# An mLSTM layer's q/k preparation: two buffers, halves, and a place inside the previous head's pipeline

## The chip, the cores and the metric

The kernel runs on the 8 cores of one Trainium2 chip. Each core computes two of the sixteen sequences on its own; nothing is exchanged. The metric is device microseconds of the slowest core.

## The reference

One layer of a hybrid decoder and a last RMSNorm. For each sequence of 2048 rows, with 1024 features:

```
x = x + 1/2 * SwiGLU_1(RMSNorm(x))
h = RMSNorm(x)
p = h @ w_in               # q, k, v, o, gates of the mLSTM; q, k, v, gates of the sparse attention
y_mlstm                    # 4 heads of 128
y_nsa                      # 8 query heads of 64: compressed, selected and window branches
x = x + concat(y_mlstm, y_nsa) @ w_out
x = x + 1/2 * SwiGLU_2(RMSNorm(x))
out = RMSNorm(x)
```

What matters here is how q and k of an mLSTM head come about, and what they are used for:

```
qk = silu(causal_conv(concat([mq, mk]), conv_w))      # 4 taps along time, each channel on its own
s  = (q . k) / sqrt(128) * exp(decay), causal          # per head, 2048 x 2048, lower triangle
h  = (s @ v) / max(|sum of s|, exp(-m))                # then a norm per head, times sigmoid(mo)
```

## The kernel before

A small scheduler of the kernel's own (`Prog`) takes instructions with the buffers that they read and write (`Buf`: the last writer and the readers since), puts each at the end of its engine's list, and waits on semaphores where one engine needs another. The order in each engine's queue is thus the order of `emit` calls in the program, and nothing moves later.

A core goes through its two sequences one after the other. Each has a feed-forward part, the mixer and a second feed-forward part, with barriers between them. The mixer (L476) first projects gates, v (`Vp`) and o (`sigmo`), then runs the four mLSTM heads, then the sparse attention, then the output projection. The change touches the mLSTM heads (L577 to L726).

A head has two parts.

*Preparation* (L611 to L625), for q and then for k: `load_w` sends 128 columns of the weights through POOL's DMA queue into one of two `wb` buffers; `proj_fm` (L529) makes four groups of eight matmuls, one group for each 512 rows of time, each into a PSUM bank; ACT copies every bank to `qpre` (fp32, 2048 columns and 3 of padding). DVE computes the four convolution taps over all 2048 columns into `cacc` (L617 once, L621 three times). ACT applies SiLU and writes `qT` or `kT` (L624). There is one `qT`, one `kT`, one `qpre` and one `cacc`. All of it stands in the program ahead of the head's pipeline.

*Pipeline* (L626 to L726): time is cut into four blocks I of 512 query rows, and for block I there are 4I + 4 steps j, one for each 128 key rows: 4 + 8 + 12 + 16 = 40 steps. At a block's first step, PE broadcasts a row of the decay in fp32 (L635), ACT copies it to `nmb` (L639), and DVE clears two accumulator banks (L643). Each step (`ml_A`) is a score matmul (L649), an Exp on ACT into `wg` (L653, ring of 4), their product `pt` on DVE (L657), and for the four diagonal steps of a block a mask on POOL (L661). The value matmuls (`ml_C`, L673) of a step are emitted LOOK = 2 steps later. At a block's end DVE copies the accumulators out (L681), and four small stages follow: s1 on DVE, s2 four squares on ACT (L702), s3 Ln and Exp on ACT, s4 on DVE (L713, and L717 four times, into `mixcat`).

Those stages come through `defer(delay, fn)`: `run_pipeline` (L512) emits `ml_A` of step t, `ml_C` of step t - 2, and then calls `tick()`, which counts every deferred function down by one and emits those that reach zero, in the order in which they were deferred. There are 42 ticks for 40 steps; what is left is emitted at the end.

`nextbank` hands out the eight PSUM banks in turn and leaves out those that are held.

Of the kernel before, what the change touches and what calls it, by code (L numbers as in the profile page):

```python
# [6 lines left out]
F32 = mybir.dt.float32  # L7
# [8 lines left out]
T = 2048  # L16
# [220 lines left out]
def build_program(nseq, debug=(), do_mixer=True):  # L237
# [46 lines left out]
    with es:  # L284
# [186 lines left out]
        def dump(name, src_ap, reads):  # L471
            if name in dbg:
                P.final_ops.append(P.emit(POOL, lambda e: e.dma_start(out=dbg[name], in_=src_ap), reads=reads, dma=True))


        def mixer(s):  # L476
# [46 lines left out]
            def load_w(name, ncols, c0=0):  # L523
                t, b = wring.next()
                src = wd[name].rearrange("(k p) m -> p k m", p=128)[:, :, c0:c0 + ncols]
                pool_cast_load(t[:, :, 0:ncols], src, [b])
                return t, b

            def proj_fm(wt, wb, c0, M, evac):  # L529
                for tg in range(4):  # L530
                    bk, bb = nextbank()
                    for k in range(8):
                        P.emit(PE, lambda e, k=k, tg=tg, bk=bk: e.matmul(  # L533
                            bk[0:M, :], lhsT=wt[:, k, c0:c0 + M], rhs=hT[:, k, tg * 512:(tg + 1) * 512],
                            start=(k == 0), stop=(k == 7)), reads=[wb, B_hT[tg]], writes=[bb])
                    evac(tg, bk, bb)
# [55 lines left out]
            wt, wb = load_w("w_mo", 512)  # L592

            def ev_o(i, bk, bb):
                st, sb_ = sgring.next()
                P.emit(ACT, lambda e: e.activation(out=st[:], in_=bk[:, :], func=AF.Sigmoid), reads=[bb], writes=[sb_])
                P.emit(DVE, lambda e: e.tensor_tensor(out=sigmo[:, i, :], in0=st[:], in1=gnbc[:], op=ALU.mult),
                       reads=[sb_, B_const], writes=[B_sig[i]])
            proj_tm(wt, wb, 0, 512, ev_o)
            P.emit(ACT, lambda e: e.activation(out=rowA[:], in_=rowA[:], func=AF.Exp), reads=[B_rA], writes=[B_rA])  # L600
            for (row, B_row, tok, B_tok) in ((rowI, B_rI, ztok, B_zt), (rowA, B_rA, ecltok, B_et)):
# [5 lines left out]
                       reads=[bb], writes=[B_tok])  # L607


            for h in range(4):  # L610
                for (wname, dstT, B_dst, cbase) in (("w_mq", qT, B_qT, 0), ("w_mk", kT, B_kT, 4)):  # L611
                    wt, wb = load_w(wname, 128, c0=h * 128)
                    P.emit(DVE, lambda e: e.memset(qpre[:, 0:3], 0.0), writes=[B_qpre])
                    proj_fm(wt, wb, 0, 128, lambda tg, bk, bb: P.emit(ACT, lambda e: e.copy(
                        out=qpre[:, 3 + tg * 512:3 + (tg + 1) * 512], in_=bk[:, :]), reads=[bb], writes=[B_qpre]))
                    cw = convw[:, cbase + h, :]
                    P.emit(DVE, lambda e, cw=cw: e.tensor_scalar(out=cacc[:], in0=qpre[:, 3:3 + T], scalar1=cw[:, 3:4],  # L617
                                                                 scalar2=None, op0=ALU.mult),
                           reads=[B_qpre, B_const], writes=[B_cacc])
                    for j in (2, 1, 0):  # L620
                        P.emit(DVE, lambda e, cw=cw, j=j: e.scalar_tensor_tensor(  # L621
                            out=cacc[:], in0=qpre[:, j:j + T], scalar=cw[:, j:j + 1], in1=cacc[:],
                            op0=ALU.mult, op1=ALU.add), reads=[B_qpre, B_cacc, B_const], writes=[B_cacc])
                    P.emit(ACT, lambda e, dstT=dstT: e.activation(out=dstT[:], in_=cacc[:], func=AF.Silu),  # L624
                           reads=[B_cacc], writes=[B_dst])  # L625
                steps = []  # L626
                for I in range(4):
                    st_I = {}
# [3 lines left out]
                def ml_A(I, j, st, h=h):  # L632
                    if j == 0:
# [8 lines left out]
                        for ab_, abb_ in accb:  # L642
# [6 lines left out]
                    P.emit(PE, lambda e, bs=bs: e.matmul(bs[:, c0:512], lhsT=kT[:, j * 128:(j + 1) * 128],  # L649
                                                         rhs=qT[:, I * 512 + c0:(I + 1) * 512], start=True, stop=True),  # L650
                           reads=[B_kT, B_qT], writes=[bbs])
# [77 lines left out]
            dump("d_qT", qT[:], [B_qT])  # L729
            dump("d_kT", kT[:], [B_kT])  # L730
            dump("d_nm", rowL[:], [B_rL])
            P.barrier()
            ar.reset(m_ar1)
# [453 lines left out]
```

How the kernel before makes its waits and increments, by code:

```python
    def replay(self, engname, eng):  # L127
        sems = self.sem_handles
        cur_wait = {}
        def wait(d):
            if cur_wait.get(d.sem, 0) >= d.val:
                return
            cur_wait[d.sem] = d.val
            eng.wait_ge(sems[d.sem], d.val)
        for op in self.ops[engname]:
            if op.is_dma and op.dma_prev is not None:
                wait(op.dma_prev)
            for d in op.deps.values():
                wait(d)
            if op.fn is None:
                continue
            ins = op.fn(eng)
            if op.is_dma:
                ins.then_inc(sems[op.sem], 16)
            elif op.waited:
                ins.then_inc(sems[op.sem], 1)
        if engname == SP:
            for o in self.final_ops:
                wait(o)
```

## Time and profile before

| | us |
|---|---|
| median of 3 runs | 5117.03 (5116.47 to 5202.21) |
| the profiled execution | 5112.91 |
| its span on the slowest core (core 7) | 5111.3 |
| spans of all cores | 5098.6 to 5111.3 |
| PE busy in the span | 3625.7 (71%) |
| DVE busy | 2238.9 (44%) |
| ACT busy | 1556.2 (30%) |
| POOL busy | 200.6 (4%) |

Times in the rows are microseconds from the first instruction of the span, on core 7. A busy time of an engine counts the time in which it executes; the end of a matmul is modelled, and matmuls overlap, so a busy PE is not a full PE. A row of a timeline merges neighbouring instructions of one form; in brackets stands how long the engine had been idle, and whose semaphore ended that. PEclk is the TensorE clock that was granted, as a share of 2.4 GHz.

### The profile page before, as it was taken

The numbers are of one execution on the slowest core, as the hardware profiler recorded it, in microseconds if no ns is written. First come the engines' busy times: TensorE is split into PE (matmuls) and PEld (weight loads), VectorE is DVE, ScalarE is ACT, GpSimd is POOL, SyncE is SP. The second block draws the span as 40 slices with busy tenths as digits, with TensorE's granted clock in tenths as the row PEclk, the third lists the DMA queues.
The fourth block names the chain that finished last, engine by engine and source line by source line (L and its number), as shares of the span: only waits on it lengthen the run. The fifth ranks groups of instructions, "written<-read, shape, count | busy, mean of one in ns | idle before, by whom it ended". The sixth has DMA issues, their size and how long they took to land.

```text
span 5111.3 us, 64455 instructions; the slowest of 8 cores (5098.6 to 5111.3 us)
## 1 busy us (share of the span) xinstructions
PE 3625.7 (71%) x19360; PEld 1709.4 (33%) x19360; DVE 2238.9 (44%) x5530; ACT 1556.2 (30%) x3053; POOL 200.6 (4%) x294
## 2 busy tenths in 40 slices
PE   3999474558575745999549993755595757459995
PEld 2444132224232323444224441322252323234442
DVE  2434335550575733343524343355506757333434
ACT  3110234441363633101130102344413636331011
POOL 0000000010000000000000000000100000000000
PEclk9999685666656558999869996856675565679997
DMA  5321110002000033130422201100110000331301
GB/s 120 42 34 25 70 21 5 5 5 31 9 2 5 1 83 58 26 50 13 97 89 42 33 13 70 21 5 5 14 23 8 1 5 1 83 58 25 50 13 66
DMA packets 147758, 169.65 MB, mean 33 GB/s; under 512 B 48828, under 2 KB 118460, under 8 KB 147424
## 3 DMA queue, kind: packets, MB, share of 16 engines
q0 software_dynamic: 124224, 101.78, 13.6%
q1 hardware_dynamic: 23200, 63.74, 3.6%
q8 instruction: 170, 2.79, 0.2%
q14 instruction: 164, 1.34, 0.1%
HBM read 225.33 MB, written 33.55 MB: 51 GB/s over the span
## 4 chain that ended last, share of the span: by engine, by line
PE 58%; DVE 16%; ACT 9%; issue 8%; DMA 7%; DVEq 1%; POOL 0%; ACTq 0%; SPq 0%; POOLq 0%
PE bank L444 12%; PE bank L448 12%; PE bank L462 11%; PE bank L533 5%; PE bank L542 3%; PE bank L978 3%; PE bank L1057 2%; PE bank L805 2%; DVE cacc L621 2%; PE bank L1011 2%; DVE hnacc L853 2%; ACT pt L986 2%; DMA xstash<-xs 2%; ACT nj L384 2%; ACT wg L653 1%
## 5 line engine op out<-in xcount | busy, mean ns | idle before, releaser
L452 ACT ACTIVATE sil<-bank 128x512 f32<-128x512 f32 x352 | 210.1, 597 | 1541.9 <-PE bank L444 1541.9
L454 DVE TENSOR_TENSOR aT<-sil,bank 128x512 bf16<-128x512 f32 x352 | 242.0, 687 | 984.8 <-PE bank L448 959.8
L444 PE MATMUL bank<-hT,w1g 128*128 128x512 bf16 x2816 | 669.9, 381 | 0.0
L448 PE MATMUL bank<-hT,w3g 128*128 128x512 bf16 x2816 | 665.3, 379 | 0.0
L462 PE MATMUL bank<-w2g,aT 128*128 128x512 bf16 x2816 | 622.6, 379 | 6.9 <-DVE xs L465 6.5
L465 DVE SCALAR_TENSOR_TENSOR xs<-bank,xs 128x512 f32<-128x512 f32 x768 | 524.1, 691 | 119.4 <-PE bank L462 82.5
L986 ACT ACTIVATE pt<-bank 128x512 bf16<-128x512 f32 (+3 forms) x1088 | 465.5, 504 | 283.3 <-PE bank L978 194.2
L396 PE MATMUL bank<-ident_b,nh 128*128 128x128 bf16 x768 | 97.1, 306 | 445.2 <-DVE nh L390 444.9
L462 PEld LDWEIGHTS bank<-w2g,aT 128*128 128x128 bf16 x2816 | 271.0, 98 | 354.6 <-issue 38.4
L444 PEld LDWEIGHTS bank<-hT,w1g 128*128 128x128 bf16 x2816 | 276.7, 98 | 334.4 <-issue 5.4
L448 PEld LDWEIGHTS bank<-hT,w3g 128*128 128x128 bf16 x2816 | 275.6, 98 | 332.6 <-issue 0.6
L533 PE MATMUL bank<-hT,wb 128*128 128x512 bf16 (+2 forms) x1408 | 337.4, 405 | 49.6 <-DMA wb<-w_mq 26.9
L649 PE MATMUL bank<-qT,kT 128*128 128x512 bf16 (+1 forms) x320 | 167.3, 539 | 171.6 <-ACT kT L624 146.3
L1011 PE MATMUL bank<-VV,pt 128*128 128x65 bf16 x3296 | 274.4, 234 | 8.6 <-DVE pt L989 3.6
L673 PE MATMUL bank<-Vp,pt 128*128 128x129 bf16 x1088 | 165.3, 294 | 156.8 <-DVE pt L657 126.2
L657 DVE SCALAR_TENSOR_TENSOR pt<-bank,wg 128x512 bf16<-128x512 f32 (+1 forms) x320 | 185.8, 608 | 184.2 <-ACT wg L653 114.8
L1011 PEld LDWEIGHTS bank<-VV,pt 128*128 128x128 bf16 x3296 | 185.7, 120 | 180.9 <-issue 166.5
L396 PEld LDWEIGHTS bank<-ident_b,nh 128*128 128x128 bf16 x768 | 74.3, 138 | 468.8 <-issue 468.8
L978 PE MATMUL bank<-nqT,ksdT 64*128 64x512 bf16 (+3 forms) x640 | 181.9, 497 | 63.2 <-DVE sm L842 35.0
L533 PEld LDWEIGHTS bank<-hT,wb 128*128 128x128 bf16 (+2 forms) x1408 | 145.2, 104 | 236.5 <-issue 93.5
L1057 PE MATMUL bank<-wout,mcT 128*128 128x512 bf16 x512 | 119.5, 388 | 128.1 <-DMA wout<-w_out 86.1
L653 ACT ACTIVATE wg<-nmb,ztok 128x512 bf16<-128x512 f32 (+1 forms) x320 | 190.3, 647 | 17.9 <-DVE pt L657 12.6
(164 smaller groups left out, 3420.8 us busy)
## 6 DMA issues: line engine op xcount, KB each, us to landing
w1g<-ffn_w POOLq DMA_DIRECT2D x20, 1024.0 KB, 10.8
w3g<-ffn_w POOLq DMA_DIRECT2D x20, 1024.0 KB, 14.9
w2g<-ffn_w POOLq DMA_DIRECT2D x20, 1024.0 KB, 8.8
xs<-x SPq DMA_DIRECT2D x32, 512.0 KB, 13.7
xstash<-xs SPq DMA_DIRECT2D x32, 512.0 KB, 2.7
out<-fo SPq DMA_DIRECT2D x32, 512.0 KB, 2.7
xs<-xstash SPq DMA_DIRECT2D x16, 512.0 KB, 14.6
xs<-xstash POOLq DMA_DIRECT2D x16, 512.0 KB, 18.1
```

Source lines behind the costliest of these rows:

```text
L444: P.emit(PE, lambda e, k=k, fc=fc, tg=tg, bu=bu, t1=t1: e.matmul(bu[:, :], lhsT=t1[:, k, fc * 128:(fc + 1) * 128], rhs=hT[:, k, tg * 512:( ...
L448: P.emit(PE, lambda e, k=k, fc=fc, tg=tg, bv=bv, t3=t3: e.matmul(bv[:, :], lhsT=t3[:, k, fc * 128:(fc + 1) * 128], rhs=hT[:, k, tg * 512:( ...
L452: P.emit(ACT, lambda e, bu=bu, st=st: e.activation(out=st[:], in_=bu[:, :], func=AF.Silu), reads=[bbu], writes=[sbf])
L454: P.emit(DVE, lambda e, fc=fc, tg=tg, st=st, bv=bv: e.tensor_tensor(out=aT[:, fc, tg * 512:(tg + 1) * 512], in0=st[:], in1=bv[:, :], op=AL ...
L462: P.emit(PE, lambda e, fc=fc, i=i, half=half, by=by, t2=t2, nfc=nfc: e.matmul(by[:, :], lhsT=aT[:, fc, i * 128:(i + 1) * 128], rhs=t2[:, f ...
L465: P.emit(DVE, lambda e, i=i, half=half, by=by: e.scalar_tensor_tensor(out=xs[:, i, half * 512:(half + 1) * 512], in0=by[:, :], scalar=0.5, ...
L533: P.emit(PE, lambda e, k=k, tg=tg, bk=bk: e.matmul(bk[0:M, :], lhsT=wt[:, k, c0:c0 + M], rhs=hT[:, k, tg * 512:(tg + 1) * 512], start=(k = ...
L653: P.emit(ACT, lambda e, wg=wg, nmb=nmb: e.activation(out=wg[:, c0:512], in_=nmb[:, c0:512], func=AF.Exp, bias=ztok[:, j, h:h + 1], scale=1.0),
L978: P.emit(PE, lambda e, bs=bs, r0=r0: e.matmul(bs[:, c0:c1], lhsT=kTt[r0:r0 + 64, j * 128:(j + 1) * 128], rhs=nqT[r0:r0 + 64, p, I * 512 + ...
L986: P.emit(ACT, lambda e, pt=pt, bs=bs: e.activation(out=pt[:, c0:c1], in_=bs[:, c0:c1], func=AF.Exp, scale=SC_N), reads=[bbs], writes=[pb])
L1011: P.emit(PE, lambda e, ab=ab, q=q, pt=pt, i=i: e.matmul(ab[:, q * 65:(q + 1) * 65], lhsT=pt[:, q * 128:(q + 1) * 128], rhs=VV[:, j, vidx, ...
L1057: P.emit(PE, lambda e, k=k, half=half, by=by, mc=mc: e.matmul(by[:, :], lhsT=mc[:, k, :], rhs=wout[:, k, half * 512:(half + 1) * 512], sta ...
```

## The change

The two parts of a head are taken apart. `prep_sched(h)` makes a list of small functions, each with an offset, that together are the preparation of head h. For head 0 they are all emitted ahead of the loop. For heads 1 to 3 they are deferred, by their offset plus 2 ticks, when the pipeline of head h - 1 begins, so that they are emitted between its steps.

- `qT` and `kT` have two buffers each; head h uses number h % 2.
- `cacc` has 1024 columns in place of 2048. Each convolution and each SiLU is done in two halves, one after the other, in the one `cacc`.
- The banks of the projection are held from the matmuls to their copy, one tick later.
- `wg` has 3 buffers in place of 4, and `sg` is gone: the sigmoid of o goes through the first 512 columns of `cacc`.

```diff
             qpre = arx.alloc("qpre", [128, T + 3], F32)
-            cacc = arx.alloc("cacc", [128, T], F32)
-            qT = arx.alloc("qT", [128, T], BF16)
-            kT = arx.alloc("kT", [128, T], BF16)
-            B_qpre, B_cacc, B_qT, B_kT = Buf(), Buf(), Buf(), Buf()
-            wgring = Ring(arx, "wg", [128, 512], BF16, 4)
-            sgring = Ring(arx, "sg", [128, 512], F32, 1)
+            cacc = arx.alloc("cacc", [128, T // 2], F32)
+            qTb = [arx.alloc(f"qT{i}", [128, T], BF16) for i in range(2)]
+            kTb = [arx.alloc(f"kT{i}", [128, T], BF16) for i in range(2)]
+            B_qTb = [Buf(), Buf()]
+            B_kTb = [Buf(), Buf()]
+            B_qpre, B_cacc = Buf(), Buf()
+            wgring = Ring(arx, "wg", [128, 512], BF16, 3)
...
+            def prep_sched(h):
+                par = h % 2
+                sched = []
+                base = 0
+                for (wname, dstT, B_dst, cbase) in (("w_mq", qTb[par], B_qTb[par], 0), ("w_mk", kTb[par], B_kTb[par], 4)):
+                    hold = {}
+                    cw = convw[:, cbase + h, :]
...
+                        hold["w"] = load_w(wname, 128, c0=h * 128)
+                        P.emit(DVE, lambda e: e.memset(qpre[:, 0:3], 0.0), writes=[B_qpre])
+                    sched.append((base, p_load))
+                    for tg in range(4):
...
+                        sched.append((base + 1 + tg, p_mm))
+                        sched.append((base + 2 + tg, p_ev))
+                    for hf in range(2):
+                        o = hf * (T // 2)
+                        s0 = base + (6 if hf == 0 else 11)
...
+                        sched.append((s0, p_c0))
+                        for n_, j in enumerate((2, 1, 0)):
...
+                            sched.append((s0 + 1 + n_, p_cj))
...
+                        sched.append((s0 + 4, p_silu))
+                    base += 17
+                return sched
+
+            for _, fn in sorted(prep_sched(0), key=lambda t: t[0]):
+                fn()
             for h in range(4):
...
+                if h + 1 < 4:
+                    for off, fn in prep_sched(h + 1):
+                        defer(off + 2, fn)
```

`p_mm` is the eight matmuls of one 512-row group, `p_ev` ACT's copy to `qpre`, `p_c0` the first tap (a tensor_scalar over 1024 columns), `p_cj` one of the three others, `p_silu` the SiLU of 1024 columns. The score matmul reads `kTb[h % 2]` and `qTb[h % 2]`.

## Rows read from the trace of the kernel before

**Rows 1.** the page's slices: granted TensorE clock in tenths, 127.8 us each

```profile
PEclk9999685666656558999869996856675565679997
```

**Rows 2.** wait list, 747 to 1141 us: waiter, releaser, us, times, longest us

```profile
PE bank L649 <- ACT kT L624: 73.2, 4, 18.6
...
DVE pt L657 <- ACT wg L653: 58.1, 38, 3.6
```

**Rows 3.** windows: us, busy PE, PEld, DVE, ACT, POOL; clock, DMA

```profile
747.06:781.79 34.73, 16.52 (x67) 6.89 (x67) 17.95 (x13) 9.81 (x12) 0.00 (x0) 0.75 0.00 0
781.79:841.18 59.39, 37.08 (x181) 18.67 (x181) 34.26 (x83) 33.71 (x75) 6.23 (x16) 0.55 0.00 1
846.50:852.50 6.00, 5.91 (x14) 2.11 (x15) 1.31 (x6) 0.74 (x2) 0.00 (x0) 0.50 0.24 24
852.50:857.00 4.50, 4.50 (x22) 2.06 (x21) 0.00 (x0) 1.46 (x3) 0.00 (x0) 1.00 0.01 4
```

**Rows 4.** timeline of ACT: start us, us, engine, line, operation [idle before, releaser]

```profile
779.74 1.91 ACT L624 ACTIVATE kT<-cacc 128x2048 bf16<-128x2048 f32 x1 [8.85 <-DVE cacc L621]
781.55 0.57 ACT L639 COPY nmb<-bank 128x512 f32<-128x512 f32 x1
782.20 1.28 ACT L653 ACT_TABLE_LOAD   x1
...
829.22 0.71 ACT L653 ACTIVATE wg<-nmb,ztok 128x512 bf16<-128x512 f32 x1
...
1079.28 1.91 ACT L624 ACTIVATE kT<-cacc 128x2048 bf16<-128x2048 f32 x1 [8.86 <-DVE cacc L621]
```

**Rows 5.** groups of instructions: busy us, mean ns, idle before

```profile
L452 ACT ACTIVATE sil<-bank 128x512 f32<-128x512 f32 x352 | 210.1, 597 | 1541.9 <-PE bank L444 1541.9
...
L390 DVE SCALAR_TENSOR_TENSOR nh<-xs,rstd,gbc 128x1024 bf16<-128x1024 f32 x96 | 119.3, 1282 | 140.7 <-DMA gbc<-mix_norm 80.9 <-DMA gbc<-ffn_norm 53.0 <-DVE rstd L376 3.5
...
L621 DVE SCALAR_TENSOR_TENSOR cacc<-qpre,convw,cacc 128x2048 f32<-128x2048 f32 x48 | 112.9, 2352 | 5.4 <-DVE cacc L617 0.5
...
L617 DVE TENSOR_SCALAR cacc<-qpre,convw 128x2048 f32<-128x2048 f32 x16 | 20.6, 1287 | 115.5 <-ACT qpre L614 115.5
```

**Rows 6.** timeline of DVE in head 0, columns as in rows 4

```profile
784.32 1.49 DVE L657 SCALAR_TENSOR_TENSOR pt<-bank,wg 128x512 bf16<-128x512 f32 x3 [3.55 <-ACT wg L653]
...
797.05 0.69 DVE L657 SCALAR_TENSOR_TENSOR pt<-bank,wg 128x512 bf16<-128x512 f32 x1 [2.37 <-ACT wg L653]
...
801.38 1.03 DVE L643 MEMSET bank<- 128x512 f32 x2
...
805.72 1.30 DVE L657 SCALAR_TENSOR_TENSOR pt<-bank,wg 128x512 bf16<-128x512 f32 x2 [3.31 <-PE bank L649]
...
823.68 1.30 DVE L657 SCALAR_TENSOR_TENSOR pt<-bank,wg 128x512 bf16<-128x512 f32 x2 [2.43 <-ACT wg L653]
...
830.09 0.69 DVE L657 SCALAR_TENSOR_TENSOR pt<-bank,wg 128x512 bf16<-128x512 f32 x1 [2.37 <-ACT wg L653]
...
833.05 2.72 DVE L657 SCALAR_TENSOR_TENSOR pt<-bank,wg 128x512 bf16<-128x512 f32 x4
...
836.87 0.69 DVE L657 SCALAR_TENSOR_TENSOR pt<-bank,wg 128x512 bf16<-128x512 f32 x1 [0.17 <-DVE pt L657]
...
840.68 0.29 DVE L657 SCALAR_TENSOR_TENSOR pt<-bank,wg 128x128 bf16<-128x128 f32 x1 [0.51 <-PE bank L649]
...
847.11 1.14 DVE L717 SCALAR_TENSOR_TENSOR mixcat<-accs,sm,sigmo 128x128 bf16<-128x128 f32 x4
```

**Rows 7.** timeline of POOL: first masks of head 0, load for head 1

```profile
785.16 1.26 POOL L661 TENSOR_TENSOR pt<-pt,trile 128x128 bf16<-128x128 bf16 x3 [42.04 <-DVE pt L657]
...
841.67 0.94 POOL L341 DMA_DIRECT2D wb<-w_mq  x1
```

**Rows 8.** timeline of PE: a row broadcast and the projections of head 1

```profile
819.83 2.07 PE L635 MATMUL bank<-rowL,sel 4*128 4x512 f32 x2
...
846.59 11.70 PE L533 MATMUL bank<-hT,wb 128*128 128x512 bf16 x40 [4.68 <-DMA wb<-w_mq]
```

More of the change, by code:

```diff
@@ L594, in ev_o @@
             def ev_o(i, bk, bb):
[L595 to L598, printed above, removed]
+                P.emit(ACT, lambda e: e.activation(out=cacc[:, 0:512], in_=bk[:, :], func=AF.Sigmoid), reads=[bb], writes=[B_cacc])
+                P.emit(DVE, lambda e: e.tensor_tensor(out=sigmo[:, i, :], in0=cacc[:, 0:512], in1=gnbc[:], op=ALU.mult),
+                       reads=[B_cacc, B_const], writes=[B_sig[i]])
             proj_tm(wt, wb, 0, 512, ev_o)
@@ L607, in mixer @@
                        reads=[bb], writes=[B_tok])
-            for h in range(4):
[L611 to L625, printed above, removed]
@@ new lines, in prep_sched, with p_load, p_mm, p_ev @@
+            def prep_sched(h):
[5 more added lines that the diff above has]
+                    cw = convw[:, cbase + h, :]
+                    def p_load(wname=wname, hold=hold):
+                        hold["w"] = load_w(wname, 128, c0=h * 128)
+                        P.emit(DVE, lambda e: e.memset(qpre[:, 0:3], 0.0), writes=[B_qpre])
+                    sched.append((base, p_load))
+                    for tg in range(4):
+                        def p_mm(tg=tg, hold=hold):
+                            wt, wb = hold["w"]
+                            bk, bb = nextbank(hold=True)
+                            for k in range(8):
+                                P.emit(PE, lambda e, k=k: e.matmul(
+                                    bk[:, :], lhsT=wt[:, k, 0:128], rhs=hT[:, k, tg * 512:(tg + 1) * 512],
+                                    start=(k == 0), stop=(k == 7)), reads=[wb, B_hT[tg]], writes=[bb])
+                            hold[("bk", tg)] = (bk, bb)
+                        def p_ev(tg=tg, hold=hold):
+                            bk, bb = hold[("bk", tg)]
+                            P.emit(ACT, lambda e: e.copy(out=qpre[:, 3 + tg * 512:3 + (tg + 1) * 512], in_=bk[:, :]),
+                                   reads=[bb], writes=[B_qpre])
+                            release(bb)
+                        sched.append((base + 1 + tg, p_mm))
[3 more added lines that the diff above has]
+                        s0 = base + (6 if hf == 0 else 11)
+                        def p_c0(o=o, cw=cw):
+                            P.emit(DVE, lambda e: e.tensor_scalar(out=cacc[:], in0=qpre[:, o + 3:o + 3 + T // 2], scalar1=cw[:, 3:4],
+                                                                  scalar2=None, op0=ALU.mult),
+                                   reads=[B_qpre, B_const], writes=[B_cacc])
+                        sched.append((s0, p_c0))
+                        for n_, j in enumerate((2, 1, 0)):
+                            def p_cj(o=o, cw=cw, j=j):
+                                P.emit(DVE, lambda e: e.scalar_tensor_tensor(
+                                    out=cacc[:], in0=qpre[:, o + j:o + j + T // 2], scalar=cw[:, j:j + 1], in1=cacc[:],
+                                    op0=ALU.mult, op1=ALU.add), reads=[B_qpre, B_cacc, B_const], writes=[B_cacc])
+                            sched.append((s0 + 1 + n_, p_cj))
+                        def p_silu(o=o, dstT=dstT, B_dst=B_dst):
+                            P.emit(ACT, lambda e: e.activation(out=dstT[:, o:o + T // 2], in_=cacc[:], func=AF.Silu),
+                                   reads=[B_cacc], writes=[B_dst])
+                        sched.append((s0 + 4, p_silu))
+                    base += 17
+                return sched
@@ L648, in ml_A @@
                     bs, bbs = nextbank()
-                    P.emit(PE, lambda e, bs=bs: e.matmul(bs[:, c0:512], lhsT=kT[:, j * 128:(j + 1) * 128],
-                                                         rhs=qT[:, I * 512 + c0:(I + 1) * 512], start=True, stop=True),
-                           reads=[B_kT, B_qT], writes=[bbs])
+                    P.emit(PE, lambda e, bs=bs: e.matmul(bs[:, c0:512], lhsT=kTb[h % 2][:, j * 128:(j + 1) * 128],
+                                                         rhs=qTb[h % 2][:, I * 512 + c0:(I + 1) * 512], start=True, stop=True),
+                           reads=[B_kTb[h % 2], B_qTb[h % 2]], writes=[bbs])
                     wg, wgb = wgring.next()
```

4 lines of the change are left out of this document (2 added, 2 removed).

## The prediction

> **What bounds the kernel now.** The page's clock row comes first [rows 1]: the change touches slices 6 to 9 and 26 to 29, where TensorE's granted clock is 5 or 6 tenths. Those are the mLSTM heads of the two sequences (four heads each, eight in all). The wait list over one sequence's heads comes next [rows 2]. The longest wait of PE with useful work behind it is for kT, the last piece of a head's preparation (73.2 us over four heads, 18 us each). Then the windows [rows 3]: the preparation of head 0 takes 34.7 us, its pipeline of 40 score steps 59.4 us. In the pipeline DVE is busy 34.3, ACT 33.7 and PE 37.1 us, and the clock is 0.55. So nobody is full, and DVE's idle 25 us look like room for the next head's preparation. The first kT and the last kT of the sequence start at 779.74 and 1079.28 [rows 4]: a head's period is 299.5/3 = 99.85 us. Of it, DVE's first to last score product (pt, 784.32 to 840.97) is 56.65 us [rows 6]; the other 43.2 us are handover, load, projection, convolution and SiLU.
>
> The timelines tell what sort of idle time it is. All five queues run in program order, and the program goes in lockstep: score matmul, wg on ACT, pt on DVE, then the value matmul two steps later. In the dense end of a head a step takes 0.86 us (0.69 of pt and 0.17 of wait at 836.87 [rows 6]), at the half clock nearly what PE needs for it. DVE's idle lies in lumps: about 3.3 us at the start of each 512-row block, and 2.37 us for wg behind four squares [rows 6].
>
> **The change, part by part.** I number the steps of a head 0 to 41. Blocks start at 0, 4, 12 and 24. The offsets plus 2 put the work here: q load after step 1; q matmuls after 2 to 5; q convolution, half by half, after 7 to 10 and 12 to 15; its SiLUs after 11 and 16; k load after 18; k matmuls after 19 to 22; k convolution after 24 to 27 and 29 to 32; SiLUs after 28 and 33. It applies to 3 heads of 4, so to 6 of 8. I follow the engine that releases pt, on the times of head 0.
>
> Removed: the 43.2 us between the last pt and the next first pt, in six places.
>
> Handover. What is left is the tail: accs, squares, Ln, Exp, four mixcat products end at 848.25, 7.3 us after the last pt; then two memsets of the next block's banks, queued behind them on DVE, 1.03 us [rows 6]. The new first pt comes 8.4 us after the last one.
>
> q load and projection. POOL works in order, and the load is queued behind the masks of steps 0 and 1. They start at 785.16, 0.84 after the first pt, and end at 786.0, 1.7 after it. From such a load's start to PE's first matmul on it is 846.59 - 841.67 = 4.9 us [rows 7, 8]; PE is in order too, so score matmul 3 waits behind the first projection matmul, and DVE runs dry. The burst now: 14 matmuls in 5.91 us at clock 0.50 (the 1.2 GHz level), the 26 after them in the rest of 11.70 us, 0.22 us each [rows 3, 8]. So 32 matmuls, the fp32 row broadcast of 2.07 us [rows 8] and some 1.7 us of score and value matmuls (diagonal ones, under two dense steps) are 13.5 + 2.1 + 1.7 = 17.3 us at half clock; 5.9 us pass at it and the rest goes twice as fast: 11.6 us. Then the last copy to qpre (0.6), the squares (2.4) and wg (0.9) come before pt 7: 3.9. Sum 1.7 + 4.9 + 11.6 + 3.9 = 22.1 from first pt to pt 7, against 797.05 - 784.32 = 12.7 now: +9.4. Block 1's own broadcast, copy and wg, which fill that stretch now, run under the burst.
>
> Costs of the halves. No row has 1024 fp32 columns of this operation from SBUF but the norm's, 1.28 us; half of the 2048-column one is 1.18 [rows 5]. I take 1.26 from start to start. The first tap is 0.64 (half of 1.287) to 1.29; I take 0.73, plus 0.1 between instructions. SiLU of 1024 columns: between 0.60 for 512 and 1.91 for 2048 [rows 4, 5], 1.03 by the line through them.
>
> First half of q (steps 7 to 11). DVE gets 0.5 more at step 7 (0.34 idle takes some) and 1.26 after each of the steps 8 to 10. The last tap ends about 805.6, with pt 11 still to come. ACT then needs table load 1.28, SiLU 1.03, nmb 0.58, the load back to Exp 1.28 [rows 4], and 0.87 from wg's start to pt's (829.22 to 830.09 [rows 4, 6]), with small gaps: pt 12 starts at 810.7, not 805.72. +5.0, nearly all of it the taps, since the boundary's idle covers the first load.
>
> Second half of q and first half of k (steps 12 to 16, 24 to 28: the same pattern). From 823.68: the first tap delays by 0.8, the second, ahead of the squares, by 1.3; the third hides in the 2.37 us wait; the fourth ends 2.1 after pt 27 starts, at 834.1. SiLU waits for it, then 1.28 + 1.03 + 1.28 + 0.87 and gaps give pt 29 at 838.7, against 833.05 [rows 6]: +5.7, twice. Behind the waiting SiLU on ACT stand wg 29 and after, and DVE waits for them; its only cover is pt 28 and the mixcat products.
>
> k load and projection (18 to 22). POOL has no mask from 12 to 19, so this load hides wholly (if not, 4.9 more). 32 matmuls and four dense steps are 13.5 + 3.4 = 16.9 to 17.1 at half clock, by the same burst 11.5 in fact, against 3.4 now: +8.1. Less 1.0, since the next broadcast runs at the higher clock: +7.1.
>
> Second half of k (29 to 33). There is no idle time here: +0.8 and three times 1.3, then DVE waits for the whole SiLU group but for one pt. From pt 29 to pt 34: 11.9 against 836.87 - 833.05 = 3.8: +8.1.
>
> Sum: 56.65 + 8.4 + 9.4 + 5.0 + 5.7 + 7.1 + 5.7 + 8.1 = 106.05 us, 6.2 above 99.85; six times, +37. The first head's preparation, now in halves over a single cacc, gains nothing and waits for SiLU at each half: +1.4, twice. Ring wg from 4 to 3: nothing, since wg is late for order and not for room [rows 2]; cacc in place of sg: nothing, one buffer each. So +40 us on the profiled 5112.9 (its span 5111.3 and 1.6 around it) is 5153; the median of the runs is 4 above that execution: 5157, and I say 5155. The work is interleaved, but each piece goes to a step where its engine is, or becomes, the last one.
>
> The Trainium skill ("ScalarE: Activation LUTs", section "What ACT_TABLE_LOAD costs") says that a switch of sets drains for 1.38 us on top of the load. This change makes 52 switches of 16; by that page the sum would be some 50 us higher, 5205. The row speaks against it: nmb ends at 782.12, the load starts at 782.20 and takes 1.28 [rows 4]. Its rule to batch calls by set is what the interleaving gives up; the load alone is in my terms.
>
> **The rivals.**
> Hidden after all (faster). The added 41 us per head fall into DVE's 25 us of idle time. For it: no engine is over 63% busy in the pipeline, and DVE waits 58 us for wg over four heads [rows 2, 3]. Against it: order within queues, above. If half of the 41 us vanish, the period is 85.5 and the time 5155 - 123 = 5032; with 30 hidden 76, and 4975. It decides from 23 us hidden per head (5155 to 5015 is 140 us, 23 a head). Below 5015: 0.10; between 5015 and 5080: 0.07.
> The clock stays down (slower). Both bursts start after starved stretches, and the pipeline's clock is 0.55 [rows 3]. If neither is raised, 17.2 in place of 11.6, twice a head: +11.2, +67 us, 5222. Against it: the burst of now rose after 14 matmuls [rows 3]. It decides where both bursts of all six heads stay low. 0.09. The other way, both at full clock from the start, is 3 us less per burst, 5119, inside the likeliest case.
> A switch of tables amid a full queue costs twice its row: 36 more at 1.28, +46, 5201. 0.04. This is the mechanism of the page named above.
> Likeliest: interleaved and not hidden, 5080 to 5215 with the last rival in it: 0.74; the middle of it, 5120 to 5190, 0.5.
>
> **How the numbers follow.** 5155 is the likeliest case. Range 5080 to 5215 leaves 0.17 below and 0.09 above; I take the low end down to 5060 for a few us per head of cover that I missed. Faster by over 2% is below 5015, slower above 5219; 2% is about what a measurement tells from no change. 0.11 faster, 0.79 within, 0.10 slower.
>
> **What would show it.** First pt to first pt about 106 us in three of four heads. Right if: DVE waits about 8 us for score matmul 3 behind a PE wait on w_mq after step 1; ACT shows 52 table loads and four DVE waits of 2 to 4 us per head behind them; the w_mk wait is gone; a DVE busier than 50 us per head. Wrong if the period is under 95: then taps or bursts were covered; over 112: then the bursts show clock 0.5 throughout, or a tap takes over 1.3 us.

## The result, and the profile after

| | before | after |
|---|---|---|
| profiled execution, us | 5112.91 | 5140.29 |
| its span on the slowest core | 5111.3 | 5138.7 |
| ratio, 95% interval | | 1.0051 (1.0037 to 1.0065) |

The change costs half a per cent, some 26 us. Executions in which the cores of a die ran slower at a lower clock are left out of every ratio and interval here; the others lie at 5114 to 5118 us before and at 5140 to 5145 after.

The page of the changed kernel, its span and its clock slices, against [rows 1]:

```profile
span 5138.7 us, 64577 instructions; the slowest of 8 cores (5123.8 to 5138.7 us)
...
PEclk9999685656656558999869996866566565579997
```

The clock pattern is that of before to a tenth or two: the change lives in slices 6 to 9 and 26 to 29 only. The wait list of core 3, the slowest, over the four heads of one sequence, 747 to 1170 us, against [rows 2] (waiter, releaser, us, times, longest):

```profile
DVE pt L699 <- ACT wg L695: 82.1, 40, 4.0
...
PE bank L691 <- ACT kT L656: 22.1, 1, 22.1
...
PE bank L627 <- DMA wb<-w_mq: 13.2, 3, 4.4
```

What the change says it does, it does: PE waits for kT once and not four times (22.1 us, before 73.2). But DVE's wait for wg has gone up from 58.1 to 82.1 us, and the wait for w_mq, 4.4 us a head, is still there. The windows of the first two overlapped periods, first pt to first pt (us, then busy PE, PEld, DVE, ACT, POOL; clock, DMA), against [rows 3]:

```profile
788.62:890.86 102.24, 52.53 (x248) 23.38 (x248) 54.47 (x114) 54.63 (x106) 11.35 (x18) 0.62 0.06 6
890.86:993.11 102.25, 52.67 (x248) 23.43 (x248) 54.44 (x115) 53.73 (x104) 11.40 (x18) 0.62 0.06 6
```

No engine is over 54% busy, and the period is 102.2 us where it was 99.3 to 101.0 in the three overlapped heads of that sequence. The work of two stretches is in one, and it takes as long as the two did. The same marks in DVE's timeline as in [rows 6]: first pt, pt 7, 12, 17, 24, 29, 34, the last one, and the next head's first:

```profile
788.62 1.50 DVE L699 SCALAR_TENSOR_TENSOR pt<-bank,wg 128x512 bf16<-128x512 f32 x3 [2.75 <-ACT wg L695]
...
811.10 0.69 DVE L699 SCALAR_TENSOR_TENSOR pt<-bank,wg 128x512 bf16<-128x512 f32 x1 [2.51 <-ACT wg L695]
...
824.16 0.69 DVE L699 SCALAR_TENSOR_TENSOR pt<-bank,wg 128x512 bf16<-128x512 f32 x1 [3.84 <-ACT wg L695]
...
839.05 1.91 DVE L699 SCALAR_TENSOR_TENSOR pt<-bank,wg 128x512 bf16<-128x512 f32 x3 [2.65 <-ACT wg L695]
...
852.75 0.69 DVE L699 SCALAR_TENSOR_TENSOR pt<-bank,wg 128x512 bf16<-128x512 f32 x1 [1.33 <-ACT wg L695]
...
867.27 0.69 DVE L699 SCALAR_TENSOR_TENSOR pt<-bank,wg 128x512 bf16<-128x512 f32 x1 [2.65 <-ACT wg L695]
...
878.56 1.99 DVE L699 SCALAR_TENSOR_TENSOR pt<-bank,wg 128x512 bf16<-128x512 f32 x3 [3.96 <-ACT wg L695]
...
882.20 0.29 DVE L699 SCALAR_TENSOR_TENSOR pt<-bank,wg 128x128 bf16<-128x128 f32 x1 [0.41 <-PE bank L691]
...
890.86 1.48 DVE L699 SCALAR_TENSOR_TENSOR pt<-bank,wg 128x512 bf16<-128x512 f32 x3
```

From these marks, [rows 6] and one more line of DVE's timeline before, that of pt 17:

```profile
815.10 1.88 DVE L657 SCALAR_TENSOR_TENSOR pt<-bank,wg 128x512 bf16<-128x512 f32 x3
```

All in us. The last column has the same marks over all six overlapped heads, after less before, on average:

| stretch | before | after | difference | forecast | mean of six heads |
|---|---|---|---|---|---|
| pt 0 to 7: q load and matmuls | 12.7 | 22.5 | +9.8 | +9.4 | +10.0 |
| 7 to 12: first half of q | 8.7 | 13.1 | +4.4 | +5.0 | +4.3 |
| 12 to 17: second half of q | 9.4 | 14.9 | +5.5 | +5.7 | +5.2 |
| 17 to 24: k matmuls | 8.6 | 13.7 | +5.1 | +7.1 | +6.2 |
| 24 to 29: first half of k | 9.4 | 14.5 | +5.2 | +5.7 | +5.2 |
| 29 to 34: second half of k | 3.8 | 11.3 | +7.5 | +8.1 | +7.5 |
| 34 to the end of the last pt | 4.1 | 3.9 | -0.2 | 0 | -0.1 |
| from there to the next head's first pt | 43.2 on average | 8.4 | -34.8 | -34.8 | -35.4 |

Head 0 is not typical in one row: its stretch 17 to 24 took 8.6 us before, and that of the five other heads 7.3 to 8.4; the mean of all six is 7.7. Over the six overlapped heads the sum is +18 us (mean period 99.7 before, 102.6 after); the two first heads' preparation adds 7 and all the rest 2: 27, the difference of the two spans.

### The profile page after: what moved, and what is told of

It reads as the page before. It is cut to its first block, busy times and chain, and to the rows that moved or that the text cites. A ratio compares the mean times of both kernels' runs of the same rounds, so it can differ in the third digit from the quotient of the medians.

```text
span 5138.7 us, 64577 instructions; the slowest of 8 cores (5123.8 to 5138.7 us)
## 1 busy us (share of the span) xinstructions
PE 3624.2 (71%) x19360; PEld 1699.0 (33%) x19360; DVE 2242.4 (44%) x5594; ACT 1604.3 (31%) x3105; POOL 218.3 (4%) x294
## 4 chain that ended last, share of the span: by engine, by line
PE 58%; DVE 15%; ACT 10%; issue 8%; DMA 7%; DVEq 1%; POOL 0%; ACTq 0%; SPq 0%; POOLq 0%
PE bank L444 12%; PE bank L448 12%; PE bank L462 11%; PE bank L533 4%; PE bank L542 3%; PE bank L1020 3%; PE bank L1099 2%; PE bank L847 2%; PE bank L1053 2%; PE bank L627 2%; DVE hnacc L895 2%; DVE cacc L650 2%; ACT pt L1028 2%; DMA xstash<-xs 2%; ACT nj L384 2%
## 5 line engine op out<-in xcount | busy, mean ns | idle before, releaser
L715 PEld LDWEIGHTS bank<-Vp,pt 128*128 128x128 bf16 x1088 | 99.3, 122 | 402.8 <-issue 392.0
L1020 PE MATMUL bank<-nqT,ksdT 64*128 64x512 bf16 (+3 forms) x640 | 181.3, 498 | 61.8 <-DVE sm L884 35.4
L533 PE MATMUL bank<-hT,wb 128*128 128x512 bf16 (+2 forms) x896 | 206.8, 395 | 22.7 <-DMA wb<-w_nq 11.8
L691 PE MATMUL bank<-qT,kT 128*128 128x512 bf16 (+1 forms) x320 | 157.1, 507 | 55.4 <-ACT kT L656 43.8
## 6 DMA issues: line engine op xcount, KB each, us to landing
w1g<-ffn_w POOLq DMA_DIRECT2D x20, 1024.0 KB, 11.5
```

The lines of the kernel that those rows point to most:

```text
L533: P.emit(PE, lambda e, k=k, tg=tg, bk=bk: e.matmul(bk[0:M, :], lhsT=wt[:, k, c0:c0 + M], rhs=hT[:, k, tg * 512:(tg + 1) * 512], start=(k = ...
L715: P.emit(PE, lambda e, ab=ab, o0=o0, pt=pt, q=q: e.matmul(ab[:, o0:o0 + 129], lhsT=pt[:, q * 128:(q + 1) * 128], rhs=Vp[:, j, h, 0:129], s ...
L1020: P.emit(PE, lambda e, bs=bs, r0=r0: e.matmul(bs[:, c0:c1], lhsT=kTt[r0:r0 + 64, j * 128:(j + 1) * 128], rhs=nqT[r0:r0 + 64, p, I * 512 + ...
```

## The experiments

Two views stand against each other. The order theory says that each piece costs by its place in an in-order queue: what it delays is read from the next pt. The rivals say that one thing eats the gain (table switches, the low clock, contention between engines), or that the pieces lie in idle time and the loss comes from elsewhere. The period of a run is the mean of first pt to first pt over its six overlapped heads.

### The halves alone

```diff
-            for _, fn in sorted(prep_sched(0), key=lambda t: t[0]):
-                fn()
             for h in range(4):
-                if h + 1 < 4:
-                    for off, fn in prep_sched(h + 1):
-                        defer(off + 2, fn)
+                for _, fn in sorted(prep_sched(h), key=lambda t: t[0]):
+                    fn()
```

> The halves alone, in the old order: every head's preparation stands ahead of its own pipeline again, but with cacc of 1024 columns, a convolution and a SiLU for each half, and wg with 3 buffers. The order theory (each piece of the new kernel costs by the place in its queue, and the halves have a price of their own) expects the price seen in the first head of the changed kernel, +3.8 us from ecltok to the first pt, at all 8 heads: +31 us, ratio 1.006 to before. The rival, that halves are as cheap as the whole and the slowdown comes from the interleaving alone, expects under +5 us, ratio 1.001.

Measured: ratio 1.0059 (1.0036 to 1.0082). A window over its first head's period:

```profile
787.26:889.95 102.69, 53.08 (x248) 25.05 (x248) 56.24 (x115) 46.77 (x99) 8.45 (x18) 0.63 0.06 6
```

102.7 us, and 103.1 on average: within half a us the period of the changed kernel. So what the change loses against before is what its halves cost, 3.4 us a head where they stand in the open, and the overlap as such is worth nothing: it takes 35 us off the gap and puts 37 into the pipeline. This run also has the three wg buffers. They are not what costs: from first pt to the end of the last a head takes 55.9 us on average here as before, and all the difference is between pipelines, 47.1 us against 43.8.

### The load of q ahead of the pipeline

```diff
-                        hold["w"] = load_w(wname, 128, c0=h * 128)
+                        hold["w"] = early.pop(h) if wname == "w_mq" and h in early else load_w(wname, 128, c0=h * 128)
...
                 if h + 1 < 4:
+                    early[h + 1] = load_w("w_mq", 128, c0=(h + 1) * 128)
                     for off, fn in prep_sched(h + 1):
```

> The changed kernel with one load moved: the next head's q weights are asked for ahead of the pipeline and not behind POOL's masks of steps 0 and 1. The order theory expects the 4.4 us for which PE waits for w_mq in every overlapped head to vanish whole, since DVE runs dry behind it: -4.4 x 6 = -26 us, about the time of before, ratio 1.000 (0.998 to 1.002). The rival, that this wait is covered by POOL, ACT and the drain of block 0, expects the time of the changed kernel, ratio 1.005.

Measured: ratio 1.0007 (0.9982 to 1.0031), period 98.9. PE's timeline in head 0 shows the first value matmuls and the q burst right behind them:

```profile
788.58 0.59 PE L718 MATMUL bank<-Vp,pt 128*128 128x129 bf16 x4 [2.94 <-DVE pt L702]
788.97 3.62 PE L629 MATMUL bank<-hT,wb 128*128 128x512 bf16 x8
```

The wait is gone, and 3.7 us a head with it, of the 4.4 expected.

### No table switch

```diff
-                            P.emit(ACT, lambda e: e.activation(out=dstT[:, o:o + T // 2], in_=cacc[:], func=AF.Silu),
+                            P.emit(ACT, lambda e: e.activation(out=dstT[:, o:o + T // 2], in_=cacc[:], func=AF.Silu if h == 0 else AF.Identity),
```

> The changed kernel with Identity in place of SiLU in the overlapped heads, so that no activation table is switched there (this leaves the SiLU of six heads out of the computation); all places and sizes stay. The order theory expects per head three groups shorter by the two table loads, 2.57 us, and the one at the block boundary by 2.1: -9.8 us a head, -59 us, 5084, ratio 0.994. The rival that the table switches are what eats the gain expects the overlap to pay once they are gone: over 17 us a head, below 5040, ratio 0.985 or less. The rival that they lie in ACT's idle time expects under 10 us in all.

Measured: ratio 0.9939 (0.9915 to 0.9963), period 92.8: -9.8 us a head, as worked out from the places. The switches are a quarter of what the pipeline got longer by (37 us, the table's rows but the last), not the whole of it.

### One tap of four

```diff
-                        for n_, j in enumerate((2, 1, 0)):
+                        for n_, j in enumerate((2, 1, 0) if h == 0 else ()):
```

> The changed kernel with only the first of the four taps in the overlapped heads (three quarters of their convolution are left out): 12 DVE instructions of 1.27 us less per head, 15.3 us of DVE time. The order theory expects most of it to be on the path, with the SiLUs no longer waiting for the last tap as well: -4.4, -3.3, -3.3 and -5 us in the four halves, -16 us a head, -96 us, 5047, ratio 0.986. The rival that the taps lie mostly in DVE's idle time, as its 44 per cent of busy time suggests, expects under -6 us a head, over 5105, ratio above 0.998.

Measured: 5080 us in a single execution (no interval), period 92.9, so -9.7 us a head and not -16, between my figure and the rival's. 15.3 us of DVE work came off; over a third of it did not shorten the period. The first fence is DVE's timeline at pt 17, the second ACT's there:

```profile
835.44 1.91 DVE L699 SCALAR_TENSOR_TENSOR pt<-bank,wg 128x512 bf16<-128x512 f32 x3 [2.40 <-ACT wg L695]
```

```profile
830.94 1.28 ACT L656 ACT_TABLE_LOAD   x1
832.24 1.06 ACT L656 ACTIVATE qT<-cacc 128x1024 bf16<-128x1024 f32 x1
833.31 1.28 ACT L695 ACT_TABLE_LOAD   x1
834.61 2.56 ACT L695 ACTIVATE wg<-nmb,ztok 128x512 bf16<-128x512 f32 x4
```

SiLU waits for no tap now, and starts as soon as wg 16 is done. Still it stands ahead of wg 17, and DVE waits 2.40 us for that, against 2.65 with the taps. The taps and the SiLU group are two chains of nearly one length; with one gone, the other sets pt 17. My expectation let both go at once.

### One matmul of eight

```diff
-                            for k in range(8):
+                            nk = 8 if h == 0 else 1
+                            for k in range(nk):
...
-                                    start=(k == 0), stop=(k == 7)), reads=[wb, B_hT[tg]], writes=[bb])
+                                    start=(k == 0), stop=(k == nk - 1)), reads=[wb, B_hT[tg]], writes=[bb])
```

> The changed kernel with one matmul of eight in each projection group of the overlapped heads (seven eighths of their projection are left out), 56 matmuls less per head. The order theory expects about 5 us less in the q burst and 5 in the k burst, the lengthening that the changed kernel's trace shows against before, less what the load's wait already covers: -10 us a head, -60 us, 5083, ratio 0.993. The rival that the bursts are hidden under ACT and DVE expects under 2 us a head, ratio above 1.002. The rival that the lower clock makes them dear expects more than 17 us a head.

Measured: ratio 0.9933 (0.9910 to 0.9957), period 93.0: -9.6 us a head. The wait for the weights stays, 4.85 us in PE's timeline:

```profile
793.98 0.59 PE L628 MATMUL bank<-hT,wb 128*128 128x512 bf16 x1 [4.85 <-DMA wb<-w_mq]
```

With seven eighths of the overlapped projection gone, all but 10 us of a 103 us period is still there. The projection is not the bound, and the low clock under it is not what eats the gain. The score and value matmuls still ran at the low clock; what a higher one would give them, no run shows.

### One SiLU group

```diff
-                            def p_cj(o=o, cw=cw, j=j):
+                            def p_cj(o=o, cw=cw, j=j, dstT=dstT, B_dst=B_dst):
+                                dst = cacc[:] if j else dstT[:, o:o + T // 2]
                                 P.emit(DVE, lambda e: e.scalar_tensor_tensor(
-                                    out=cacc[:], in0=qpre[:, o + j:o + j + T // 2], scalar=cw[:, j:j + 1], in1=cacc[:],
...
+                                    out=dst, in0=qpre[:, o + j:o + j + T // 2], scalar=cw[:, j:j + 1], in1=cacc[:],
...
-                            P.emit(ACT, lambda e: e.activation(out=dstT[:, o:o + T // 2], in_=cacc[:], func=AF.Silu),
-                                   reads=[B_cacc], writes=[B_dst])
-                        sched.append((s0 + 4, p_silu))
...
+                        P.emit(ACT, lambda e: e.activation(out=dstT[:], in_=dstT[:], func=AF.Silu),
+                               reads=[B_dst], writes=[B_dst])
+                    sched.append((32, p_silu))
```

> The full computation: the last tap writes q or k in bf16, and SiLU is applied in place, q and k together after step 33, so 2 table loads per overlapped head in place of 8. The order theory expects -3.2 us at step 11, -2.65 at steps 16 and 28 each, +2.8 after step 33 where the one group is 6.5 us long, in sum -5.7 us a head, -34 us, and -3 for the first heads, whose convolution waits for no SiLU now: 5106, ratio 0.998. The rival that the number of switches is what costs expects -6 x 1.28 us a head and more, -46 us or more beside the first heads: below 5095.

Measured: ratio 0.9964 (0.9946 to 0.9982), 5094 to 5095 us, period 95.7: -6.9 a head, and the first head's preparation is 3.5 to 4 us shorter. The time is the rival's figure (below 5095) as much as mine plus a miss of 12; this run alone does not tell the number of switches from their places, and it also lets a half's taps start without waiting for the SiLU of the half before. The run without switches prices the loads: 8 of them, all gone, gave 9.8.

### Load and tail

Against the run before:

```diff
-                    sched.append((32, p_silu))
+                    sched.append((38, p_silu))
...
+                    early[h + 1] = load_w("w_mq", 128, c0=(h + 1) * 128)
```

> The full computation: the early q load and the in-place SiLUs of the two runs before, with the SiLU group emitted after step 39 and not 33, where ACT has been seen idle for 4.8 us between the last wg and the squares. The order theory expects -26 (load), -37 (one group), and about -5 us a head for the place, -30: 5050, ratio 0.987. The rival that only the amount of work on an engine counts and not its place expects the last step to bring nothing: 5080, ratio 0.993.

Measured: ratio 0.9881 (0.9861 to 0.9900), period 89.0. That is 6.7 below 95.7: by the marks, the stretch with the q load is 5.0 shorter and pt 29 to 34, which held the SiLU group, 3.6, and the handover is 2.0 longer. If the load is worth its 3.7 here too, the place of the SiLU group is worth 3.0 and not the 5 expected. ACT's timeline at a head's end:

```profile
862.02 1.28 ACT L659 ACT_TABLE_LOAD   x1
863.32 1.91 ACT L659 ACTIVATE qT<-qT 128x2048 bf16<-128x2048 bf16 x1
865.13 1.89 ACT L659 ACTIVATE kT<-kT 128x2048 bf16<-128x2048 bf16 x1
866.93 0.39 ACT L748 ACTIVATE mjunk<-accs,sm 128x128 f32<-128x128 f32 x1
...
869.25 1.28 ACT L753 ACT_TABLE_LOAD   x1
```

The group begins when the last wg is done. The squares' input is ready at 866.15 and they start at 866.93: the group holds them up by 0.7 us or so. With the load back, 1.28 us and now ahead of Ln, that makes the handover 10.3 us and not 8.4.

### Slots for everything

The same pieces as in the run before, each after a step behind which the traces show its engine idle. The k load goes ahead of the pipeline too, qpre is tracked by quarters, so that a tap waits for the copies it reads and no others, and its first three columns are cleared once a sequence and not once a projection:

```diff
-                        sched.append((base + 1 + tg, p_mm))
-                        sched.append((base + 2 + tg, p_ev))
+            MM = {"w_mq": [0, 1, 4, 6], "w_mk": [12, 14, 16, 18]}
+            TAPS = [3, 3, 3, 6, 11, 11, 11, 14, 23, 23, 23, 26, 26, 28, 30, 32]
+            SILU = 39
...
+                        sched.append((s, p_mm))
+                        sched.append((s + 1, p_ev))
```

> The full computation, with every piece put where the trace shows its engine idle: both loads ahead of the pipeline; q matmuls after steps 0, 1, 4 and 6, k matmuls after 12, 14, 16 and 18; taps in threes after steps 3, 11 and 23 (block boundaries, DVE idle for 3.3 us) and single ones after 6, 14 and 26 (behind them the wait for the squares), the last three after 28, 30 and 32; q and k SiLU in place after step 39; qpre tracked by its four column groups. The order theory expects a head's period of pipeline 56.7, handover 8.4, exposed SiLU 1.6, exposed taps 5, half of the k burst 3.5 and some 3 of rest: 78 us against 99.85, -22 x 6 = -131 us: 4985, ratio 0.974 (0.968 to 0.982). The rival that overlap on this chip is lost to contention between engines whatever the place expects 5050 or more, as in the run before.

Measured: ratio 0.9688 (0.9669 to 0.9707), 4952 to 4954 us, period 75.2. Not all of it comes from places: in the first heads, where nothing overlaps, the finer tracking and the early k load take 6 us off the preparation against the run before. A window over one period:

```profile
854.08:927.92 73.84, 49.32 (x248) 22.36 (x247) 54.82 (x114) 45.25 (x97) 10.76 (x18) 0.73 0.08 8
```

DVE is at 74% and does as much as in the changed kernel (54.8 us against 54.5). Its timeline at the boundary to block 2 shows three taps and two memsets where there was a wait, and pt 12 right behind them:

```profile
872.09 0.74 DVE L651 TENSOR_SCALAR cacc<-qpre,convw 128x1024 f32<-128x1024 f32 x1
872.94 2.69 DVE L658 SCALAR_TENSOR_TENSOR cacc<-qpre,convw,cacc 128x1024 f32<-128x1024 f32 x2
875.73 1.02 DVE L697 MEMSET bank<- 128x512 f32 x2
876.66 0.67 DVE L711 SCALAR_TENSOR_TENSOR pt<-bank,wg 128x512 bf16<-128x512 f32 x1
```

### The old order with early loads

```diff
-                    wt, wb = load_w(wname, 128, c0=h * 128)
+                    wt, wb = early.pop(wname) if wname in early else load_w(wname, 128, c0=h * 128)
...
+                if h + 1 < 4:
+                    for wname in ("w_mq", "w_mk"):
+                        early[wname] = load_w(wname, 128, c0=(h + 1) * 128)
```

> The kernel of before with one thing moved: the next head's two weight loads are asked for ahead of the pipeline, the preparation stays where it was. The order theory expects PE's wait of 4.7 us for w_mq to vanish in the six later heads, since nothing else lies behind it there: -28 us, ratio 0.9945. So a part of what the slots kernel gains needs no overlap at all. The rival, that the tail of the head before (squares, Ln, Exp, mixcat) sets the start of the preparation anyway, expects under 2 us a head, ratio 0.998 or more.

Measured: ratio 0.9950 (0.9930 to 0.9969), period 95.1. PE's timeline between two heads, 64 projection matmuls right behind the last value matmul:

```profile
842.57 15.66 PE L533 MATMUL bank<-hT,wb 128*128 128x512 bf16 x64
```

Against [rows 8], where PE idled for 4.68 us before them. Two loads moved in the kernel of before do better than the whole change (0.9950 against 1.0051).

### Matmuls in slots, taps in rows

Against the slots kernel. One group of k's matmuls stands a step later, too:

```diff
-            MM = {"w_mq": [0, 1, 4, 6], "w_mk": [12, 14, 16, 18]}
+            MM = {"w_mq": [0, 1, 4, 6], "w_mk": [12, 15, 16, 18]}
-            TAPS = [3, 3, 3, 6, 11, 11, 11, 14, 23, 23, 23, 26, 26, 28, 30, 32]
+            TAPS = [7, 8, 9, 10, 12, 13, 14, 15, 24, 25, 26, 27, 29, 30, 31, 32]
```

> The slots kernel with its taps back at one per step (after steps 7 to 10, 12 to 15, 24 to 27, 29 to 32, as in the changed kernel), its matmuls still after 0, 1, 4, 6 and 12, 15, 16, 18, early loads and the SiLU group after step 39. It splits the 13.7 us a head between the run with early load and tail SiLU (period 88.9) and the slots kernel (75.2). The order theory expects the taps' places to be worth about 3.3 us idle at each of three block boundaries less what is lost in the memsets behind, 7 to 8 us, and the matmuls' places the rest, 6: period 83, about 5015, ratio 0.980. The rival that only the matmuls' places count, since PE with its low clock is the one that starves the others, expects the slots kernel's time, ratio 0.969.

Measured: ratio 0.9736 (0.9717 to 0.9756), 4976 to 4978 us, period 78.5. A window over one period:

```profile
858.38:936.20 77.82, 49.99 (x247) 23.26 (x251) 54.29 (x114) 46.59 (x98) 11.30 (x18) 0.70 0.07 8
```

So of the 13.8 us between 89.0 and 75.2 the matmuls' places (with the early k load and the finer tracking of qpre) are worth 10.5 and the taps' 3.3 (with that one group a step apart). I had given the taps 7 to 8; the rival gave all to the matmuls and is the nearer one. Whether PE's clock has a part in it stays open: it is 0.70 here and 0.63 with load and tail, with PE busy 50 and 53 us. Two of q's four groups now run in the handover, while DVE works off the tail of the head before. By the marks, the stretch with the q matmuls (pt 0 to 7) went from 17.9 us to 12.1 and the one with the k matmuls (17 to 24) from 14.5 to 8.0, while the two stretches between them got 1.9 longer. So the k groups, none of which is in the handover, gained as much as q's; how the 10.5 divides between places and tracking, no run tells.

## Why the prediction came out as it did

**The sign and the size.** Forecast: 5155 against a median of 5117, +0.74%, with 0.79 for less than 2% either way. Measured: +0.51%. The range held the time, and the change is inside 2%; but the forecast step, 38 to 40 us, is nearly half again as large as the measured 26 to 27, and the move that I filed under "within 2%" is clear of its own interval. To call it no change would be wrong.

**The step that failed.** The mechanism held; terms of the sum were mis-sized, and their errors partly cancelled. The largest single one is the low clock's 5.9 us in the k burst: it lasted 2.8 in head 0, and the stretch from pt 17 to 24 came to 14.0 us on average and not 15.7. The four halves came to 2.2 us less than forecast, the q burst to 0.7 more. The whole period is 102.6 us and not 106.05, six times 3.4 too high. Against it, the first heads' preparation cost 3.7 us each and not 1.4. That the total missed by 13 us only is owed in part to these opposite errors.

**The bound.** Right. The added work did not fall into idle time; the run with halves alone has the same period. In head 0, on whose times I had worked, seven of the table's eight rows follow the forecast within 0.6 us; over six heads all eight do within 0.9.

**Handover, 8.4.** Right to 0.1.

**q load and projection, +9.4.** +9.8. The load waits behind two masks. From its start to the first matmul on it, it is 4.6 us and not 4.9, and PE waits for 4.4 of them. DVE runs dry for 8.68 us:

```profile
798.79 0.29 DVE L699 SCALAR_TENSOR_TENSOR pt<-bank,wg 128x128 bf16<-128x128 f32 x1 [8.68 <-PE bank L715]
```

PE's timeline of the bursts (q first, then k):

```profile
795.11 3.45 PE L627 MATMUL bank<-hT,wb 128*128 128x512 bf16 x8 [4.38 <-DMA wb<-w_mq]
...
798.62 1.89 PE L627 MATMUL bank<-hT,wb 128*128 128x512 bf16 x8
...
805.55 1.89 PE L627 MATMUL bank<-hT,wb 128*128 128x512 bf16 x8 [1.39 <-DVE accs L723]
...
840.27 3.08 PE L627 MATMUL bank<-hT,wb 128*128 128x512 bf16 x8
...
843.63 1.89 PE L627 MATMUL bank<-hT,wb 128*128 128x512 bf16 x8
```

The first eight of q take 3.45 us at the low clock, the next eight 1.89. I had put the rise after 14 matmuls, from one burst of before [rows 3]; here it came after eight. The stretch still took more than forecast, and one cause is in the rows: the last group waits 1.39 us for a PSUM bank that DVE's accs copies set free, which I had not seen.

**k projection, +7.1.** +5.1 in head 0, +6.2 on average. The mis-sized term is the low clock's 5.9 us. The first eight matmuls of k took 3.08 us and the rest ran at 1.89 per eight. A window from PE's first instruction after its wait (columns as in [rows 3]):

```profile
839.88:842.60 2.72, 2.72 (x10) 1.27 (x11) 1.08 (x3) 0.89 (x2) 0.00 (x0) 0.50 0.02 6
```

From 842.9 the clock is 1.00. In all six overlapped heads it rose within eight matmuls of k. With 2.8 us in place of 5.9, my own sum gives 9.9 us for the burst and not 11.5, 1.6 of the 1.7 us by which the stretch of the changed kernel came out shorter. I had taken 14 matmuls from one burst of before [rows 3]. The other seven heads of before had 7 to 14, so I had taken the longest; I can give no reason from these traces why k's bursts rose sooner. Both kinds of burst start after PE has waited, 4.68 us in [rows 8] and 3.64 here. The rest of the difference between the forecast +7.1 and the mean of +6.2 is in before: its 8.6 us for this stretch, which I read in head 0, are 7.7 on average.

**The four halves, +5.0, +5.7, +5.7, +8.1.** 4.4, 5.5, 5.2, 7.5: 1.9 too much in sum. The durations of the instructions were right, as the rows by form of the changed kernel show (busy us, mean ns):

```profile
L650 DVE SCALAR_TENSOR_TENSOR cacc<-qpre,convw,cacc 128x1024 f32<-128x1024 f32 x96 | 122.7, 1278 | 2.9 <-DVE cacc L650 0.5
...
L656 ACT ACT_TABLE_LOAD x26 | 33.4, 1283 | 79.9 <-DVE cacc L650 79.9
...
L644 DVE TENSOR_SCALAR cacc<-qpre,convw 128x1024 f32<-128x1024 f32 x32 | 23.9, 747 | 34.6 <-ACT qpre L634 26.8 <-ACT qT L656 5.2 <-ACT kT L656 2.6
```

A tap takes 1.28 (1.26 from start to start taken), the first one 0.75 (0.73), and there are 52 loads of tables in the heads, 26 each way. From start to start it is less than I took: a tap that starts at 869.13 pushes the next pt to 870.33, one at 870.93 to 872.12, 1.2 us and not 1.26 to 1.3. Over twelve taps that is near 1 us of the 1.9; the rest is not resolved. ACT's timeline at step 16 is the chain of the forecast, piece by piece:

```profile
834.55 1.28 ACT L656 ACT_TABLE_LOAD   x1 [1.03 <-DVE cacc L650]
835.85 1.06 ACT L656 ACTIVATE qT<-cacc 128x1024 bf16<-128x1024 f32 x1
836.92 1.28 ACT L695 ACT_TABLE_LOAD   x1
838.21 2.56 ACT L695 ACTIVATE wg<-nmb,ztok 128x512 bf16<-128x512 f32 x4
```

The Trainium skill ("ScalarE: Activation LUTs", section "What ACT_TABLE_LOAD costs") adds a drain of 1.38 us to each switch. The trace does not show it: SiLU starts 0.02 us after its load ends and the load back 0.01 us after SiLU, and the run without switches gave 9.8 us for eight loads, 1.2 us each. Its advice to batch calls by set (section "Table sets: the hidden batching unit") agrees with the run with one group per head, 6.9 us a head, in which the places changed too.

**The first head, +1.4 twice.** +3.8 and +3.6, 5 us in all that go the other way. DVE's timeline there:

```profile
764.85 0.75 DVE L644 TENSOR_SCALAR cacc<-qpre,convw 128x1024 f32<-128x1024 f32 x1 [2.60 <-ACT qT L656]
...
773.58 0.75 DVE L644 TENSOR_SCALAR cacc<-qpre,convw 128x1024 f32<-128x1024 f32 x1 [3.61 <-ACT qpre L634]
774.43 4.06 DVE L650 SCALAR_TENSOR_TENSOR cacc<-qpre,convw,cacc 128x1024 f32<-128x1024 f32 x3
...
779.82 0.76 DVE L644 TENSOR_SCALAR cacc<-qpre,convw 128x1024 f32<-128x1024 f32 x1 [1.32 <-ACT kT L656]
```

2.60 and 1.32 us are the waits of a half for the SiLU of the half before, over the single cacc. Behind them 2.9 us come back: the last SiLU of q and of k is 0.85 shorter, and q's table load, 1.28, is already done. What is left, 1.0, is within the 1.4 that I had. I left out that the taps themselves are dearer in halves: 4.9 us for a half from its first tap to its last (5.3 in the first), against 8.7 for the whole [rows 5], 2.7 us in all. Back to back, taps on one cacc start 1.39 us apart, not 1.26.

**The last head, 0.** +1.6 in one sequence and nothing in the other. The pipelines of before differ among themselves by as much, 55.1 to 57.1 us, so this is no effect of the change that could be told.

**Rivals.** "Hidden after all" fell at once. "The clock stays down" too: it rose sooner than I said. The dear switch is excluded by the rows of ACT at step 16.

In sum: six periods 3.4 us too high (106.05 against 102.6, half of it in the k burst), less 1 us since before's mean is 99.7 and not 99.85, less 2.3 in each first head and 2 in the rest, makes the 13 us between the forecast +40 and the measured +27.

## What to carry to other kernels

In a program of in-order queues like this one, an engine that is half idle had room where its idle lumps were, and little elsewhere. List each engine's waits by the step behind which they fall, and put there pieces of just that length. Spread evenly, the pieces gave nothing here. The slots kernel took 27 us off a period of 103, but not by places alone: an early load (3.7 where it was tried by itself), one SiLU group in place of four (6.9), its place at the tail (some 3), the matmuls' places with the finer tracking (10.5) and the taps' places (3.3). Before an overlap is built, look for the one wait it would also carry along: moving two DMA issues in the old kernel gained as much as the whole change cost, half a per cent.

## What the runs showed of the hardware

POOL's mask of a 128x128 bf16 tile took 0.42 to 0.43 us in every instance in the heads before [rows 7]. In the changed kernel it takes three times as long where it meets a tap on DVE. POOL's timeline (the first beside a tap, the second beside none):

```profile
813.20 1.33 POOL L703 TENSOR_TENSOR pt<-pt,trile 128x128 bf16<-128x128 bf16 x1 [13.54 <-DVE pt L699]
...
844.59 0.41 POOL L703 TENSOR_TENSOR pt<-pt,trile 128x128 bf16<-128x128 bf16 x1 [23.77 <-DVE pt L699]
```

In the changed kernel and in the one with matmuls in slots, 18 masks each begin during one of the three later taps; they take 1.04 to 1.33 us and end 0.28 us after the tap. The Trainium skill ("SBUF — State Buffer", section "Who interferes with whom") says that a DVE instruction with two SBUF inputs contends with a GpSimd one that reads SBUF; the taps L650 have two such inputs, and the trace agrees. The first tap has one SBUF input and holds a mask up just the same. With one tap of four no mask met a tap, but in the slots kernel 18 masks begin during a first tap, and they too end 0.28 us after it. DVE's timeline and POOL's there:

```profile
856.50 0.74 DVE L651 TENSOR_SCALAR cacc<-qpre,convw 128x1024 f32<-128x1024 f32 x1
```

```profile
856.72 0.80 POOL L715 TENSOR_TENSOR pt<-pt,trile 128x128 bf16<-128x128 bf16 x1 [0.35 <-DVE pt L711]
```

The six masks that were already running when a first tap began took 0.43 us. The weight of all this is small here: PE's waits for masks went from 14.2 to 19.4 us over four heads. I had not counted it.
